# The chunk mask of the attention as a 97th row of queries and keys, in place of a VectorE memset of the scores

## The chip, the cores and the metric

The kernel runs on one core of a Trainium2 chip. The metric is the device time of one execution in microseconds (us), as the median of several runs. TensorE (PE in the profile, PEld for its weight loads), VectorE (DVE), ScalarE (ACT), GpSimd (POOL) and the queue that issues DMAs (SP) run side by side and meet at semaphores.

## The reference, cut to what matters

One layer: RMS norm, a combined projection, three groups of heads side by side (a gated delta rule, a pooling, a softmax attention), an output projection, and a SwiGLU. The change touches only the attention, 4 heads over 1024 tokens with queries and keys of 96 elements:

```python
for qs in range(0, s, Q_BLOCK):                     # Q_BLOCK = 128
    end = qs + Q_BLOCK
    scores = einsum('bqhd,bkhd->bhqk', qf[:, qs:end], kf[:, :end])
    mask = (arange(end) // CHUNK)[None, :] <= ((qs + arange(Q_BLOCK)) // CHUNK)[:, None]    # CHUNK = 64
    p = softmax(where(mask, scores, -inf), axis=-1)
    outs.append(einsum('bhqk,bkhd->bqhd', p, vf[:, :end]))
```

A tile of 128 queries sees all keys up to its own end, except that its first 64 queries must not see its last 64 keys.

## The kernel before, in words

The program is written by hand, engine by engine; what runs beside what is set by the order of the code on each engine and by semaphores. It has four parts: the input projection with its preparations (to about 322 us of the span), four rounds of attention and delta rule (325 to 567 us), the output projection, and the SwiGLU.

A **round** computes one attention head and two chunks of the delta rule. A list `ORDER`, the same for every engine, interleaves the stages of both; the first round is unrolled (`FIRST_ROUND`), rounds 2 to 4 are a loop of each engine (`Fori`). In a round the attention goes through the eight query tiles t = 7 down to 0. A tile's scores have (t + 1) x 128 key columns and lie in two banks of PSUM (4 and 5):

- stage `att_s`: PE multiplies the tile's 96 rows of `qh` by those of `kT` (L2140), in one matmul for up to 512 keys, in two above; every float32 matmul shows as two passes in the trace. VectorE then writes -1e30 into the 64 x 64 corner of the scores (memset, L1756), takes the row maximum (L1758) and negates it (L1760). ScalarE takes the exponential with that bias (L1241, with the row sum).
- stage `att_t`: PE transposes the probabilities by groups of four key tiles (L2156), ScalarE copies them to SBUF (L1247).
- stage `att_pv`: PE multiplies them by V (L2168), VectorE divides by the row sum (L1764, L1767).

The matmuls of L2067 and L2072, and VectorE's L1692 to L1744, are the delta rule's. L2088 opens a chunk of it. `sig` and `gafter` are the signal after an instruction and the wait for a named one: VectorE's maximum waits for the memset's signal (`mask{t}`), since the engine's own writes are to be waited for too.

Ahead of the rounds, POOL sets `n_base` (L948, L949), on which VectorE's small triangular inverses (L1633, L1636) start; these end where the rounds begin for VectorE. Rows 0 to 95 of `kT` are loaded once (`kT_loaded`), those of `qh` once for each head.

Of the kernel before, what the change touches and what calls it, by code (L numbers as in the profile page):

```python
# [30 lines left out]
P = 128  # L31
QK = NOPE + ROPE
# [41 lines left out]
def hybrid_block(nc, e_d, a_d, diag_d, n_d, qkv_d, qk_d, x2_d, hid_d, hs_d, wt_d, x, positions, attn_norm, w_in, conv_w, a_log, dt_bias, gdn_out_norm, pool_w, pool_scale,  # L74
# [206 lines left out]
    with ctx:  # L281
        def sem(name):
            return ctx.enter_context(nc.semaphore(name))
# [71 lines left out]
        qkv_kept = [sem(f"qkv_kept{s}") for s in range(2)]  # L355
        qk_kept = [sem(f"qk_kept{s}") for s in range(2)]
        kT_loaded = sem("kT_loaded")
        pool_moved = sem("pool_moved")
        lat_squared = sem("latents_squared")
        lat_summed = sem("latents_summed")  # L360
# [29 lines left out]
        for t in q_tiles:  # L390
            for g in groups_of[t]:
                head_part.append(("att_t", (t, g), 0))
                if t > 0 and g == groups_of[t][-1]:
# [5 lines left out]
                   ahead=True)  # L399
        td = Steps(sem("att_dve"), [f"{n}{w if st == 'att_s' else w[0]}" for st, w, _ in head_part  # L400
                                    if st == "att_s" or st == "att_pv" and w[1] == groups_of[w[0]][-1]
                                    for n in (("mask", "rowmax", "max") if st == "att_s" else ("rinv", "o"))],
                   ahead=True)


# [18 lines left out]
        def heads_of(m):  # L424
            return m[:, :].unsqueeze(1).broadcast_to([P, 4, P])
# [457 lines left out]
        def _(pool):  # L883
# [52 lines left out]
            for pair in PREP_AT.values():  # L936
                for c in pair:
                    if c >= 2:
                        pool.wait_ge(decay_summed, c - 1)
                    pool.tensor_tensor(gtg[c % 2][:, :, :], heads_of(gt), per_head(g_log[:, c, :]), ALU.mult).then_inc(gtg_ready, 1)  # L940
                for c in pair:
                    pool.wait_ge(key_ss, c + 1)
                    pool.tensor_tensor(k_len[:, c, :], k_ss[c % 2][:, 0, :], half_pos[:, 0:4], ALU.pow).then_inc(key_len, 1)
                for c in pair:
                    pool.wait_ge(decay_exp, c + 1)
                    pool.tensor_tensor(pE[c % 2][:, :, :], pE[c % 2][:, :, :], heads_of(le), ALU.mult).then_inc(decay_masked, 1)
            pool.wait_ge(raw_used, M_GATE + 2)
            link(pool.memset(n_base[:, :, :], 0.0))  # L948
            pool.memset(n_base[:, :, :].rearrange("p i j -> p (i j)")[:, 0:BASE * BASE:BASE + 1], 1.0).then_inc(n_started, 1)  # L949
# [435 lines left out]
        def _(dve):  # L1385
# [43 lines left out]
            def sig(c, ins):  # L1429
                ins.then_inc(c.sem, 1)  # L1430
# [232 lines left out]
            def stages(order, rnd):  # L1663
# [7 lines left out]
                for stage_name, b, back in order:  # L1671
# [30 lines left out]
                    elif stage_name == "yz1":  # L1702
                        gafter(gp[b], "y1")
                        gsig(dve.tensor_tensor(n_[:, 1, :, :], n_[:, 0, :, :], bank_w, ALU.subtract))
                        gafter(gp[b], "z1")
                        gsig(dve.tensor_tensor(m_[:, :, :], m_[:, :, :], bank_u, ALU.subtract))
                    elif stage_name == "yz2":
                        gafter(gp[b], "y2")
                        gsig(dve.tensor_tensor(n_[:, 0, :, :], n_[:, 1, :, :], bank_w, ALU.subtract))
                    elif stage_name == "ks":  # L1710
                        gafter(gp[b], "ks")
                        gsig(dve.tensor_tensor(e[:, :, :], bank_u, per_head(decay(0, b)), ALU.mult))
                        own("r0")
                        gsig(dve.tensor_tensor(e[:, :, :], Vn[b][:, :, :], e[:, :, :], ALU.subtract))
                        gafter(gp[b], "qs")
                        gsig(dve.tensor_tensor(bm[:, :, :], bank_w, per_head(decay(0, b)), ALU.mult))
                    elif stage_name == "tr":
                        gafter(gp[b], "tr")
                        gsig(dve.tensor_tensor(a[:, :, :], bank_u, per_head(
                            k_inv[:, chunk_at, :].rearrange("p a h -> p (a h)")), ALU.mult))  # L1720
                    elif stage_name == "av":
                        gafter(gp[b], "ds")
                        gafter(gg[b], "sd")
                        gsig(dve.tensor_tensor(S_[:, :, :], S_[:, :, :], bank_w, ALU.add))
                        own("o1")
                        gsig(dve.tensor_tensor(m_[:, :, :], bm[:, :, :], bank_u, ALU.add))
                    elif stage_name == "oms":

                        gafter(ga[b], "osq")
                        gsig(dve.tensor_reduce(sc[:, 24:28], Vn[b][:, :, :], axis=AX.X, op=ALU.add))  # L1730
                        own("osum")
                        gsig(dve.scalar_tensor_tensor(sc[:, 28:32], sc[:, 24:28], 1.0 / GDN_DIM, sc[:, 36:40],
                                                      ALU.mult, ALU.mult))
                        own("oms0")
                        gsig(dve.tensor_scalar(sc[:, 28:32], sc[:, 28:32], EPS, None, ALU.add))
                    elif stage_name == "on":
                        gafter(gg[b], "pow")
                        gsig(dve.tensor_tensor(sc[:, 40:44], sc[:, 32:36], sc[:, 12:16], ALU.mult))
                        own("of")
                        gsig(dve.tensor_tensor(n_[:, 1, :, :], m_[:, :, :], per_head(sc[:, 40:44]), ALU.mult))  # L1740
                    elif stage_name == "ot":
                        gafter(gp[b], "ot")
                        tile = ds(i * (2 * P) + b * P, P)
                        gsig(dve.scalar_tensor_tensor(oT[:, ds(i * 2 + b, 1), 0:4, :].rearrange("p t k n -> p (t k) n"),  # L1744
                                                      bank_u, cols[:, C_GDN:C_GDN + 1], sgT[:, :, tile],
                                                      ALU.mult, ALU.mult))
                    elif stage_name == "att_s":
                        t, w = b, (b + 1) * P
                        gafter(tp, f"s{t}")
                        if t < TT - 1:  # L1750
                            gafter(ta, f"e{t + 1}")
                        else:
                            gafter(ta, "e0", i - 1)
                        s2 = ps[:, 4:6, :].rearrange("p a n -> p (a n)")

                        sig(td, dve.memset(s2[0:CHUNK, w - CHUNK:w], BIG_NEG))  # L1756
                        gafter(td, f"mask{t}")
                        sig(td, dve.tensor_reduce(row_stats[t % 2][:, 3:4], s2[:, 0:w], axis=AX.X, op=ALU.max))  # L1758
                        gafter(td, f"rowmax{t}")
                        sig(td, dve.tensor_scalar(row_stats[t % 2][:, 0:1], row_stats[t % 2][:, 3:4], -1.0, None, ALU.mult))  # L1760
                    elif stage_name == "att_pv" and b[1] == groups_of[b[0]][-1]:
                        t = b[0]
                        gafter(ta, f"e{t}")
                        sig(td, dve.reciprocal(row_stats[t % 2][:, 2:3], row_stats[t % 2][:, 1:2]))  # L1764
                        gafter(td, f"rinv{t}")
                        gafter(tp, f"pv{t}.{b[1]}")
                        sig(td, dve.tensor_scalar(V[:, t, ds(i, 1), :].rearrange("p a d -> p (a d)"),  # L1767
                                                  ps[:, 7, 0:V_DIM], row_stats[t % 2][:, 2:3], None, ALU.mult))
                    elif stage_name == "w_low":
                        k, half = ds(i * 2 + b // 2, 1), slice(b % 2 * BANK, (b % 2 + 1) * BANK)  # L1770
                        dve.wait_ge(w_out_high, i * 4 + (b + 1))
                        dve.tensor_tensor(w_out_lo[:, k, half].rearrange("p a n -> p (a n)"),
                                          w_out_sb[:, k, half].rearrange("p a n -> p (a n)"),
                                          w_out_hi[:, k, half].rearrange("p a n -> p (a n)").bitcast(f32),
                                          ALU.subtract).then_inc(w_out_ready, 1)
# [127 lines left out]
        def _(pe):  # L1903
# [153 lines left out]
            for c_ in (gp[0], gp[1], tp):  # L2057
                pe.sem_inc(c_.sem, len(c_.names))
            pe.wait_ge(kT_loaded, 16)
            def stages(order, rnd):  # L2060
                def gafter(c, name, rnd=None):
                    pe.wait_ge(c.sem, c.after(name, i if rnd is None else rnd))
# [12 lines left out]
                for stage_name, b, back in order:  # L2075
# [55 lines left out]
                    elif stage_name == "att_s":  # L2131
# [4 lines left out]
                        else:  # L2136
                            gafter(ta, f"e{t + 1}")
                        for h in range(-(-w // BANK)):
                            n = min(BANK, w - h * BANK)
                            last = pe.matmul(ps[:, 4 + h, 0:n], qh[0:QK, t * P:(t + 1) * P],  # L2140
                                             kT[0:QK, ds(i, 1), h * BANK:h * BANK + n].rearrange("p a n -> p (a n)"),
                                             start=True, stop=True)
                        last.then_inc(tp.sem, 1)
                    elif stage_name == "att_t":
                        t, g = b
# [184 lines left out]
```

## Time and profile before

| | us |
|---|---|
| median of 3 runs | 1325.63 |
| lowest and highest | 1322.32, 1327.6 |
| the profiled execution's own time | 1325.09 |
| its span in the trace | 1322.8 |
| PE busy | 1256.4 (95%) |
| VectorE busy | 834.3 (63%) |
| ScalarE busy | 471.1 (36%) |
| POOL busy | 400.0 (30%) |

The span runs from the first to the last instruction; 2.3 us of the profiled execution's time lie around it. An engine's busy time doesn't say what bounds a stage: that is read from the waits and from the chain of work that ended last, which follows each step back to what released it.

### The profile page before, as it was taken

To read this page: it belongs to the slowest core of one execution; us is meant where nothing else is said; L and a number is where in the kernel's file an instruction comes from. 1 tells how busy PE (TensorE), PEld (TensorE's weight loads), DVE (VectorE), ACT (ScalarE), POOL (GpSimd) and SP (SyncE) were. 2 spreads that over 40 slices of the span, in tenths; PEclk is the share of its full clock that TensorE was granted. 3 is DMA by queue.
4 is the path that set the end of the run, shared out by engine and by line. 5 is a ranking of instruction groups with operands and counts; after the bars stand their busy time and mean duration, and the time that the engine had idled before them with its cause. 6 is when DMAs were issued, how large, how long until landed. Compare 5 with 4: busy or idle time off the path is not lost.

```text
span 1322.8 us, 17456 instructions
## 1 busy us (share of the span) xinstructions
PE 1256.4 (95%) x6156; PEld 1038.5 (79%) x6156; DVE 834.3 (63%) x1324; ACT 471.1 (36%) x776; POOL 400.0 (30%) x367
## 2 busy tenths in 40 slices
PE   6999999998898988899979999999999998999998
PEld 6787777886787776778867888888888886888887
DVE  5446877877365656645385566556655668686776
ACT  5232223342333333324344333333333343344342
POOL 5001111430121112100463655666566445200000
PEclk9998999999798889999989999999999998999999
DMA  7311333537531212004212665565468339575644
GB/s 222 111 49 32 111 97 104 175 121 200 178 85 51 77 50 60 0 9 167 96 54 85 204 199 192 175 222 176 149 215 281 127 97 314 179 234 138 200 118 169
DMA packets 188982, 182.64 MB, mean 138 GB/s; under 512 B 19486, under 2 KB 145772, under 8 KB 188908
## 3 DMA queue, kind: packets, MB, share of 16 engines
q1 hardware_dynamic: 188784, 181.64, 43.6%
q8 instruction: 44, 0.72, 0.2%
q14 instruction: 30, 0.25, 0.1%
q10 hardware_dynamic: 124, 0.04, 0.0%
HBM read 123.97 MB, written 56.62 MB: 137 GB/s over the span
## 4 chain that ended last, share of the span: by engine, by line
PE 69%; DVE 17%; issue 6%; ACT 3%; POOL 2%; DMA 1%; SPq 0%; DVEq 0%; ACTq 0%; POOLq 0%
PE ps L2284 31%; PE ps L2289 14%; PE ps L2067 5%; PE ps L2197 5%; PE ps L1944 4%; PE ps L2140 3%; DVE stage L1545 2%; PE ps L2168 2%; PE ps L1922 2%; DVE w_lo L1426 1%; PE ps L2156 1%; DVE row_stat L1758 1%; DVE wop_lo L1825 1%; DVE stage L1539 1%; POOL mla_sc L931 1%
## 5 line engine op out<-in xcount | busy, mean ns | idle before, releaser
L2284 PE MATMUL ps<-xop,wop_hi 128*128 128x512 f32 x1232 | 381.3, 391 | 6.9 <-issue 4.3
L2284 PEld LDWEIGHTS ps<-xop,wop_hi 128*128 128x128 f32 x1232 | 231.9, 189 | 56.8 <-issue 6.2
L2284 PE MATMUL ps<-xop,wop_lo 128*128 128x512 f32 x616 | 240.4, 390 | 0.0
L2289 PE MATMUL ps<-dop,wop_hi 128*128 128x512 f32 x440 | 137.4, 394 | 6.2 <-DVE x L1897 6.2
L2284 PEld LDWEIGHTS ps<-xop,wop_lo 128*128 128x128 f32 x616 | 116.1, 188 | 24.3
L1825 DVE TENSOR_TENSOR wop_lo<-w_sumS,wop_hi 128x512 fp32r<-128x512 f32 (+1 forms) x104 | 86.6, 835 | 72.4 <-ACT wop_hi L1306 72.4
L1825 DVE TENSOR_TENSOR wop_lo<-w_pair,wop_hi 128x512 fp32r<-128x512 f32 (+1 forms) x78 | 85.2, 1096 | 38.6 <-ACT wop_hi L1306 38.6
L1897 DVE TENSOR_TENSOR x<-x,ps 128x512 f32<-128x512 f32 x112 | 76.6, 684 | 44.3 <-PE ps L2289 44.2
L1944 PE MATMUL ps<-act_hi,w_hi 128*128 128x512 f32 x320 | 104.3, 407 | 0.2 <-DVE stage L1545 0.2
L2289 PEld LDWEIGHTS ps<-dop,wop_hi 128*128 128x128 f32 x440 | 82.9, 190 | 25.7 <-DVE wop_lo L1825 5.8
L1944 PE MATMUL ps<-act_lo,w_hi 128*128 128x512 f32 x320 | 99.5, 392 | 0.0
L1944 PE MATMUL ps<-act_hi,w_lo 128*128 128x512 f32 x320 | 99.5, 392 | 0.0
L2289 PE MATMUL ps<-dop,wop_lo 128*128 128x512 f32 x220 | 86.3, 392 | 0.0
L1306 ACT ACTIVATE wop_hi<-w_sumS 128x512 fp32r<-128x512 f32 (+1 forms) x104 | 63.3, 609 | 63.4 <-PE ps L2284 41.2
L1944 PEld LDWEIGHTS ps<-act_hi,w_hi 128*128 128x128 f32 x320 | 60.3, 191 | 16.2 <-issue 4.7
L1944 PEld LDWEIGHTS ps<-act_lo,w_hi 128*128 128x128 f32 x320 | 60.8, 190 | 13.0
L1944 PEld LDWEIGHTS ps<-act_hi,w_lo 128*128 128x128 f32 x320 | 60.6, 189 | 12.8
L1306 ACT ACTIVATE wop_hi<-w_pair 128x512 fp32r<-128x512 f32 (+1 forms) x78 | 47.4, 612 | 65.0 <-PE ps L2284 53.7
L1426 DVE TENSOR_TENSOR w_lo<-raw,w_hi 128x1024 fp32r<-128x1024 f32 x20 | 27.0, 1350 | 59.4 <-ACT w_hi L1121 59.4
L1025 POOL TENSOR_TENSOR w_sumS<-w_pair 128x512 f32<-128x512 f32 (+1 forms) x26 | 33.6, 1291 | 74.8 <-DVE wop_lo L1825 61.9
L1241 ACT ACTIVATE probs<-ps,row_stat 128x1024 f32<-128x1024 f32 (+7 forms) x32 | 23.7, 741 | 89.9 <-DVE row_stat L1760 89.9
L2168 PEld LDWEIGHTS ps<-V,probsT 128*128 128x128 f32 x288 | 39.8, 206 | 14.4 <-issue 6.8
(308 smaller groups left out, 2340.5 us busy)
## 6 DMA issues: line engine op xcount, KB each, us to landing
w_pair<-in_w_gate_up SPq DMA_DIRECT2D x44, 512.0 KB, 5.3
hidden<-up SPq DMA_DIRECT2D x22, 512.0 KB, 3.0
wd_rows<-in_w_down SPq DMA_DIRECT2D x22, 512.0 KB, 5.4
raw<-in_w_in SPq DMA_DIRECT2D x21, 512.0 KB, 4.4
wd_raw<-down_sums SPq DMA_DIRECT2D x12, 768.0 KB, 8.2
down_sums<-wd_rows SPq DMA_DIRECT2D x33, 256.0 KB, 2.6
wd_raw<-in_w_down SPq DMA_DIRECT2D x9, 768.0 KB, 7.1
qkv_kept<-qkv_st SPq DMA_DIRECT2D x12, 512.0 KB, 5.3
```

The costliest lines, as they stand in the source:

```text
L1025: pool.tensor_tensor(s1, a21, a22, ALU.add).then_inc(sums_ready, 1)
L1306: act.activation(wop_hi[q % RING][:, 0:kh, :], src, ACT.Copy).then_inc(wop_high, 1)
L1426: dve.tensor_tensor(w_lo[slot][:, :, :], raw[rawslot][:, :, :], w_hi[slot][:, :, :].bitcast(f32), ALU.subtract).then_inc(raw_used, 1)
L1825: dve.tensor_tensor(wop_lo[q % RING][:, 0:kh, :], src, wop_hi[q % RING][:, 0:kh, :].bitcast(f32), ALU.subtract).then_inc(wop_ready, 1)
L1897: dve.tensor_tensor(part, part, bank, ALU.add).then_inc(added, 1)
L1944: last = pe.matmul(ps[0:rows, pair + h, :], w[:, k, 0:rows], a[:, k, h * BANK:(h + 1) * BANK], start=(k == 0 and w is whi and a is a_hi), ...
L2067: last = pe.matmul(ps[:, out_bank, h * P:(h + 1) * P], lhs(h), rhs(h), start=True, stop=True)
L2140: last = pe.matmul(ps[:, 4 + h, 0:n], qh[0:QK, t * P:(t + 1) * P], kT[0:QK, ds(i, 1), h * BANK:h * BANK + n].rearrange("p a n -> p (a n)") ...
L2168: last = pe.matmul(ps[:, 7, 0:V_DIM], probsT[0][:, j, :], V[:, kt, ds(i, 1), :].rearrange("p a d -> p (a d)"), start=(kt == 0), stop=(kt = ...
L2197: last = pe.matmul(ps[:, op_pair[t] + h, :], o, w[:, k, h * BANK:(h + 1) * BANK], start=(k == 0 and len(parts) == 2 and w is w_out_hi), st ...
L2284: last = pe.matmul(ps[:, bank, :].rearrange("p (t n) -> p t n", n=P), w[:, k, :], a[:, k, :, :], start=(p in ("P1", "P2", "P7") and k == 0 ...
L2289: last = pe.matmul(ps[:, bank, :], w[:, k, :], a[:, k, :], start=(p in ("P1", "P2", "P7") and k == 0 and w is wop_hi[s] and a is hi), stop ...
```

## The change

The mask becomes part of the product. Row 96 of `kT` is set to 0 for the first 64 and to -1e30 for the last 64 keys of every tile, row 96 of `qh` to 1 for the first 64 and to 0 for the last 64 queries. The product of a query tile with its own key tile (the diagonal block, 128 x 128) then takes 97 rows in place of 96, which adds 1 x -1e30 in just the masked corner. Keys ahead of the diagonal block are still multiplied with 96 rows, so the scores of a tile now come from matmuls over the t x 128 earlier keys and one over the last 128. The memset on VectorE and the wait for it fall away. POOL fills the two rows once, ahead of `n_base`; PE waits for them ahead of the rounds.

```diff
+            k_halves = kT[QK:QK + 1, :, :].rearrange("p h (t c) -> p (h t) c", c=P)
+            q_halves = qh[QK:QK + 1, :].rearrange("p (t c) -> p t c", c=P)
+            pool.wait_ge(mla_turned, TT)
+            pool.wait_ge(decay_masked, TT)
+            link(pool.memset(k_halves[:, :, 0:CHUNK], 0.0))
+            pool.memset(k_halves[:, :, CHUNK:P], BIG_NEG).then_inc(mask_rows, 1)
+            pool.wait_ge(mask_rows, 1)
+            link(pool.memset(q_halves[:, :, 0:CHUNK], 1.0))
+            pool.memset(q_halves[:, :, CHUNK:P], 0.0).then_inc(mask_rows, 1)
+            pool.wait_ge(mask_rows, 2)
             pool.wait_ge(raw_used, M_GATE + 2)
             link(pool.memset(n_base[:, :, :], 0.0))
...
-                        sig(td, dve.memset(s2[0:CHUNK, w - CHUNK:w], BIG_NEG))
-                        gafter(td, f"mask{t}")
                         sig(td, dve.tensor_reduce(row_stats[t % 2][:, 3:4], s2[:, 0:w], axis=AX.X, op=ALU.max))
...
             pe.wait_ge(kT_loaded, 16)
+            pe.wait_ge(mask_rows, 2)
...
                         for h in range(-(-w // BANK)):
-                            n = min(BANK, w - h * BANK)
-                            last = pe.matmul(ps[:, 4 + h, 0:n], qh[0:QK, t * P:(t + 1) * P],
-                                             kT[0:QK, ds(i, 1), h * BANK:h * BANK + n].rearrange("p a n -> p (a n)"),
-                                             start=True, stop=True)
+                            n = min(BANK, t * P - h * BANK)
+                            if n > 0:
+                                pe.matmul(ps[:, 4 + h, 0:n], qh[0:QK, t * P:(t + 1) * P],
+                                          kT[0:QK, ds(i, 1), h * BANK:h * BANK + n].rearrange("p a n -> p (a n)"),
+                                          start=True, stop=True)
+                        at = t * P % BANK
+                        last = pe.matmul(ps[:, 4 + t * P // BANK, at:at + P], qh[0:QK + 1, t * P:(t + 1) * P],
+                                         kT[0:QK + 1, ds(i, 1), t * P:w].rearrange("p a n -> p (a n)"), start=True, stop=True)
                         last.then_inc(tp.sem, 1)
```

On PE, in the loop of rounds 2 to 4, the order of instructions around tile 7 before the change is this. `ISA` and `REGISTER_ALU` are register operations of the engine's sequencer, in brackets stand the semaphores that a row waits for (`att_act` is ScalarE's in the attention):

```order
L2134 ISA
L2062 ISA [waits head_loaded]
L2140 ISA [waits att_act]
L2140 MATMUL ps<-kT_89,qh_290 128x512
L2140 ISA
L2140 MATMUL ps<-kT_89,qh_290 128x512
L2062 REGISTER_ALU
L2062 REGISTER_ALU [waits gdn_dve0]
L2067 MATMUL ps<-S_299,qkvf1_291 128x128 [waits gdn_dve1]
```

And this after it:

```order
L2144 ISA
L2072 ISA [waits head_loaded]
L2151 ISA [waits att_act]
L2151 MATMUL ps<-kT_89,qh_290 128x512
L2151 ISA
L2151 MATMUL ps<-kT_89,qh_290 128x384
L2155 ISA
L2155 MATMUL ps<-kT_89,qh_290 128x128
L2072 REGISTER_ALU
```

The second 512 keys are split into 384 and 128, with a register operation between them. The same split comes in tiles 6, 5, 3, 2 and 1; in tile 4 (512 and 128 keys before too) and in tile 0 the number of matmuls stays.

On VectorE, at the same tile of the loop, before (`row_stat` holds the row statistics, `att_pe` and `att_dve` are PE's and VectorE's own semaphores in the attention):

```order
L1665 ISA [waits att_pe]
L1756 MEMSET ps 64x64 [waits att_act]
L1665 ISA
L1758 TENSOR_REDUCE row_stat1_74<-ps 128x1 [waits att_dve]
L1665 REGISTER_ALU
L1760 TENSOR_SCALAR row_stat1_74<-row_stat1_74 128x1 [waits att_dve]
L1665 ISA
```

And after:

```order
L1676 ISA
L1676 ISA [waits att_pe]
L1767 TENSOR_REDUCE row_stat1_74<-ps 128x1 [waits att_act]
L1769 TENSOR_SCALAR row_stat1_74<-row_stat1_74 128x1 [waits att_dve]
L1676 ISA
```

The memset and its wait are gone, the maximum takes over the waits for PE and ScalarE, and two register operations go with them. The order of all other work on VectorE, and all of it on ScalarE and in the DMA queue, stays.

## Rows read from the trace of the kernel before

**Rows 1.** The page: the span, and each engine's busy time, share and instructions.

```profile
span 1322.8 us, 17456 instructions
PE 1256.4 (95%) x6156; PEld 1038.5 (79%) x6156; DVE 834.3 (63%) x1324; ACT 471.1 (36%) x776; POOL 400.0 (30%) x367
```

**Rows 2.** Windows: busy time and count by engine, granted clock (PEclk), DMA share, GB/s.

```profile
280.00:325.00 45.00, 43.02 (x190) 34.20 (x189) 31.24 (x70) 14.41 (x15) 5.58 (x6) 1.00 0.53 146
325.00:386.00 61.00, 49.00 (x311) 41.63 (x310) 32.55 (x90) 19.87 (x42) 9.89 (x8) 0.83 0.52 160
386.00:447.00 61.00, 54.02 (x363) 46.56 (x363) 35.97 (x89) 20.06 (x42) 11.55 (x10) 0.91 0.21 59
447.00:507.00 60.00, 53.18 (x355) 45.59 (x353) 35.63 (x87) 20.07 (x42) 11.50 (x10) 0.90 0.21 59
507.00:567.00 60.00, 51.21 (x359) 43.69 (x359) 36.97 (x90) 20.64 (x44) 11.54 (x10) 0.94 0.09 26
```

**Rows 3.** Waits, 328 to 567 us: who waited for whom, total, times, longest.

```profile
ACT probs L1241 <- DVE row_stat L1760: 89.9, 32, 6.9
DVE ps L1756 <- PE ps L2140: 55.9, 15, 9.1
PE ps L2156 <- ACT probs L1241: 17.9, 16, 5.0
```

**Rows 4.** The chain of work that ended last, second round: start, us, what.

```profile
386.58 2.24 PE ps L2140 x4
...
389.13 1.24 DVE row_stat L1758
...
391.99 0.65 PE ps L2156 x4
```

**Rows 5.** The same chain: first and last of 23 row maxima on it.

```profile
329.68 1.24 DVE row_stat L1758
...
562.39 0.30 DVE row_stat L1758
```

**Rows 6.** VectorE in order of time, second round, two tiles.

```profile
388.98 0.11 DVE L1756 MEMSET ps<- 64x64 f32 x1 [2.46 <-PE ps L2140]
389.13 1.23 DVE L1758 TENSOR_REDUCE row_stat<-ps 128x1 f32<-128x1024 f32 x1
...
428.33 0.11 DVE L1756 MEMSET ps<- 64x64 f32 x1
428.47 0.69 DVE L1758 TENSOR_REDUCE row_stat<-ps 128x1 f32<-128x512 f32 x1
```

**Rows 7.** The chain, 420 to 450 us: scores of tiles 3, 2, 0, 7.

```profile
426.24 0.86 PE ps L2140 x2
432.82 0.66 PE ps L2140 x2
441.43 0.24 PE ps L2140 x2
446.31 3.62 PE ps L2140 x4
```

**Rows 8.** Weight loads around tile 4 of the first round (512 and 128 keys).

```profile
359.26 0.19 PEld L2140 LDWEIGHTS ps<-kT,qh 96*128 96x128 f32 x1 [0.24 <-issue]
359.69 0.19 PEld L2140 LDWEIGHTS ps<-kT,qh 96*128 96x128 f32 x1 [0.24 <-issue]
359.80 0.53 PEld L2168 LDWEIGHTS ps<-V,probsT 128*128 128x128 f32 x4
```

**Rows 9.** Line L2140 with count: least/median/most ns, first and last start, forms.

```profile
L2140 PEld LDWEIGHTS ps<-kT,qh x96: 188/191/338, 325.0 to 561.7; 96*128 96x128 f32 x96
...
L2140 PEldq FUSED_REGOPS  x6: 51/51/51, 386.2 to 506.9; - x6
```

**Rows 10.** POOL and then VectorE ahead of the rounds, in order of time.

```profile
291.67 0.95 POOL L948 MEMSET n_base<- 128x1024 f32 x1
...
304.42 0.21 DVE L1633 TENSOR_TENSOR solve_tmp<-u_base,n_base 128x31 f32<-128x31 f32 x1 [9.68 <-DMA u_base<-blocks_kept]
```

More of the change, by code:

```diff
@@ L357, in hybrid_block @@
         kT_loaded = sem("kT_loaded")
+        mask_rows = sem("mask_rows")
         pool_moved = sem("pool_moved")
@@ L401, in hybrid_block @@
                                     if st == "att_s" or st == "att_pv" and w[1] == groups_of[w[0]][-1]
-                                    for n in (("mask", "rowmax", "max") if st == "att_s" else ("rinv", "o"))],
+                                    for n in (("rowmax", "max") if st == "att_s" else ("rinv", "o"))],
                    ahead=True)
```

## The prediction

> **What bounds the kernel now.** I read the page first: PE is busy for 95% of the span [rows 1], so time is lost or won only where PE waits or where it gets more work. The change acts in the four rounds, so I read the windows next, cut at the rounds. In the four of them PE is busy for 49.00, 54.02, 53.18 and 51.21 us of 61, 61, 60 and 60, which leaves 34.6 us in which it stands; in the 45 us ahead of them it leaves only 2 us, and VectorE is busy for 33 to 37 us of each round [rows 2]. So neither engine is full in the rounds: the reader is to see a relay, in which one waits for the other in turn.
>
> The waits say at which hand-over. ScalarE's exponential waits for VectorE's negated maximum 32 times, once for each of the 8 tiles of 4 heads, and PE's transpose L2156 waits for the exponential 16 times, 17.9 us in total, which is half of PE's idle time [rows 3]. VectorE in turn waits 15 times for the score product, at the very memset that the change removes [rows 3]. The chain that ended last shows the relay with its parts: score matmuls 386.58 to 388.82, maximum at 389.13 to 390.37 with the memset just ahead of it, then the exponential's start-up, transposes at 391.99 [rows 4]. Over the four rounds the chain goes through a row maximum 23 times out of 32, between the two of [rows 5]. In the other 9 the maximum is ready early enough, and PE works on the delta rule meanwhile.
>
> **The change part by part.**
>
> *The memset goes.* It lasts 0.11 us [rows 6]. What leaves the relay is the distance from its start to the start of the maximum, since the maximum now starts where the memset did, on the same signals of PE and ScalarE: 0.15 us at 389 us and 0.14 at 428 us [rows 6], whether VectorE had stood idle before it or not. I take 0.145. On the 23 places of the chain [rows 5] that is 23 x 0.145 = 3.3 us. Upper end: all 32, 4.6 us. Lower end: only the 16 at which PE's own row shows the wait for the exponential [rows 3], 2.3 us. I take the chain's 3.3, because it also counts the places where the memset delays the delta rule's work that stands behind it on VectorE. The two register operations that go with it lie ahead of and beside the maximum; the distance above is the same with and without an idle spell before it [rows 6], so I give them nothing. At most they would save as much again as one such operation shows on PE, 0.051 us [rows 9], in 24 looped tiles: 1.2 us.
>
> *The last 128 keys get a matmul of their own.* The columns that PE streams stay the same; six tiles in each head have one matmul more, 24 in all, or 48 passes of [rows 9]'s kind. The trace has all the sizes that a split needs: 512 keys in one matmul took 0.86 us, 384 took 0.66, 128 took 0.24 [rows 7]. Cut in two it is 0.66 + 0.24 = 0.90 in place of 0.86, 0.04 us dearer. The weight loads give a lower price: tile 4 has 512 and 128 keys already, and its loads start 0.43 and then 0.11 us apart [rows 8], which is 512 to 128 with nothing added. I take the middle, 0.02 us for a split, 24 x 0.02 = 0.5 us; ends 0 and 1.0. All of it goes to PE, which is on the chain at most of these places, so nothing hides it.
>
> *One row more in the product.* No row of the trace has a 97-row matmul. Nearest is the change from 128 rows (L2088, L2067, L2168) to 96 and back, which happens at every tile; in [rows 8] the load for L2168 follows the last 96-row one after 0.11 us, no more than a pass of 128 columns. I take 0; the other end is the first rival below.
>
> *A register operation between the matmuls, in the loop.* One for each of six tiles in three rounds, 18 times, 0.051 us each [rows 9]: 0.9 us if PE stood still for it. It stands behind a matmul of at least 128 columns, whose two passes take 0.24 us [rows 7], so PE is still streaming while its sequencer does it. I take 0; upper end 0.9.
>
> *POOL fills the two rows.* Four memsets, 2048 and 2048 elements on one partition of `kT`, 512 and 512 of `qh`. The nearest row fills 1024 elements of each partition in 0.95 us [rows 10], so 5120 elements are about 4.8 us. They stand ahead of `n_base` on POOL, whose memset ended at 292.62 (a small one follows); VectorE first uses it at 304.42, when a DMA released it [rows 10]. That leaves up to 11.8 us of cover, which 4.8 don't fill; if POOL took 3.5 us per 1024 elements in place of 0.95 (17.5 us in all), the inverses and with them VectorE's start in the rounds would come 5.7 us late. Nothing else is queued behind them on POOL before the rounds, and PE's new wait for the rows is long over at 325 us. I take 0.
>
> *Sum.* -3.3 + 0.5 = -2.8 us. Against the profiled execution (1325.09, of which 1322.8 span and 2.3 around it) that is 1322.3; against the median of 1325.63, which lies 0.5 above it, **1322.8 us**. With the ends: at most -4.6 - 1.2 = -5.8, at least -2.3 + 1.0 + 0.9 = -0.4.
>
> **The rivals.** No change that can be measured is anything within 0.5%, 6.6 us, of before; the forecast lies inside it.
>
> *Exposed weight loads (slower).* The split works only if the weight load for the 128-column matmul, and the step from 96 to 97 rows, hide behind the matmul before. If each of the 64 passes of a diagonal block had to wait for its weight load of 0.19 us [rows 9] (32 tiles, two passes), it would be +12.2 us, with -3.3 a net +8.9: 1334.5. It counts as slower once a pass pays more than (6.6 + 3.3) / 64 = 0.15 us. Against it: within L2140 a load of 0.19 us starts before the 0.43 us pass ahead of it is done, for the same 96 rows [rows 8]. For it: no row shows 97 rows. 0.07.
> The Trainium skill (TensorE: Matmul & The Clock Gate, Part 3, The mechanism) says that a weight load overlaps running matmuls only when their row groups differ; by that rule 96 and 97 rows share groups, each added load would be paid, and the outcome would be this rival's. The trace does not agree: loads and matmuls of the same 96 rows overlap in it. The same page elsewhere lets loads go ahead into a background buffer, which is what the rows look like.
>
> *The gain is taken up elsewhere.* A tile's exponential comes 0.145 us earlier, but what PE does next waits for another signal that was as late, for instance the delta rule's results from VectorE. Then only the cost of the split is left: 0 to +1.9, about 1326. For it: 23 steps of a chain are shortened by little each, and a chain that is second by less than 0.145 us takes over. Against it: the waits at L2156 last 1.1 us on average (17.9 us in 16 [rows 3]). 0.17.
>
> *The clock.* In the rounds the granted clock is 0.83, 0.91, 0.90 and 0.94 on average, against 1.00 ahead of them [rows 2], a mix of the two levels, 2.4 and 1.2 GHz, and it is lowest in the round in which PE was busy least (49.00 us of 61). Where it is low, work of PE doubles: tile 7's scores took 3.62 us in one round and 2.24 in another [rows 4, 7], 1.4 us apart. A step earlier or later by 0.145 us can put such a stretch beside other work, in either direction. Three stretches' worth less would be -2.8 - 4.2 = -7.0, 1318.6, which counts as faster: 0.08. As much more would be +1.4, 1327.0, still no change: 0.06. For it: the four rounds do the same work and differ in clock by 0.83 to 0.94, and the three runs of before differ by 5.3 us. Against it: nothing in the change pushes it one way.
>
> *It doesn't do what it says.* The memset is gone from VectorE's order for certain; only a POOL fill that runs slower than 2.3 us per 1024 elements, and so past its cover, would undo the gain (5120 elements in 11.8 us). Little chance, 0.01.
>
> **How the numbers follow.** The forecast (-5.8 to -0.4) has 0.61, the taken-up gain 0.17, the clock 0.08 down and 0.06 up, exposed loads 0.07, the late POOL 0.01. Faster by over 0.5% are the clock downward and 0.02 of the forecast's upper end together with a smaller help of the clock: 0.10. Slower is the exposed loads: 0.07. The rest, 0.83, is no change. The range leaves out the exposed loads and half of the clock's tails: from 1318.6 to 1327.2.
>
> **What the changed kernel's profile would show.** VectorE's maximum waits for PE where the memset did, 32 times, with no memset row. The distance from the end of tile 7's last score pass to the maximum's start, 0.31 us before (388.82 to 389.13 [rows 4]), is about 0.17. PE has 48 passes more; on the chain, tile 3's scores take 0.86 to 0.90 us at full clock and tile 0's stay at 0.24. The loads of the 97-row passes start 0.11 us apart, with no gap of 0.19 us on PE ahead of the pass. POOL's four memsets end before 300 us, and VectorE's inverses still start on the DMA. PE's wait at L2156 for the exponential shrinks by some 2 us. The prediction is wrong if the rounds together become shorter by over 6 us without a change in the granted clock, if 97-row passes stand apart from their neighbours, or if the inverses start late.

## The result and the profile after

The changed kernel takes 1313.0 us (median of 6, 1312.68 to 1315.31), the one before 1326.09 (6 runs, 1320.22 to 1329.46). The ratio is 0.9913, 95% interval 0.9891 to 0.9934: faster by 13.1 us, 0.9%. Forecast were 1322.8 us and a range from 1318.6 to 1327.2; the result lies below it.

The page of the changed kernel, to be read against [rows 1]:

```profile
span 1311.2 us, 17485 instructions
PE 1250.3 (95%) x6204; PEld 1039.2 (79%) x6204; DVE 829.6 (63%) x1292; ACT 471.2 (36%) x776; POOL 404.9 (31%) x371
```

TensorE has 48 passes more, VectorE 32 instructions fewer. The four new memsets on POOL took 4.7 us, as estimated, and `n_base` was set long before VectorE's inverses, which a DMA still released. In order of time, POOL and then VectorE, against [rows 10]:

```profile
291.21 1.81 POOL L952 MEMSET kT<- 1x2048 f32 x1
293.08 1.81 POOL L953 MEMSET kT<- 1x2048 f32 x1
294.95 0.52 POOL L955 MEMSET qh<- 1x512 f32 x1
295.53 0.52 POOL L956 MEMSET qh<- 1x512 f32 x1
296.10 0.96 POOL L959 MEMSET n_base<- 128x1024 f32 x1
...
303.85 0.21 DVE L1644 TENSOR_TENSOR solve_tmp<-u_base,n_base 128x31 f32<-128x31 f32 x1 [9.75 <-DMA u_base<-blocks_kept]
```

The chain of the changed kernel at tile 7 of the second round, against [rows 4] (L2151 are the scores of the earlier keys, L2155 of the last 128; L1767 is the maximum, L1769 the negation):

```profile
384.43 1.61 PE ps L2151 x4
386.04 0.24 PE ps L2155 x2
...
386.40 1.24 DVE row_stat L1767
387.64 0.02 issue
387.66 0.17 DVE row_stat L1769
...
389.27 0.65 PE ps L2170 x4
```

The last pass of the scores ends at 386.28 and the maximum starts at 386.40, 0.12 us later; before it was 388.82 to 389.13, 0.31 us. The saving at this tile is 0.19 us, not the 0.145 between the starts of memset and maximum in [rows 6]: the memset also started later behind its release than the maximum does. The signs of the prediction that speak of waits hold too: TensorE's waits at the transposes for the exponential went from 17.9 us ([rows 3]) to 15.2.

The new passes don't stand apart. Weight loads around tile 4 in the second round, against [rows 8]:

```profile
412.90 0.19 PEld L2155 LDWEIGHTS ps<-kT,qh 97*128 97x128 f32 x1 [0.24 <-issue]
413.33 0.19 PEld L2155 LDWEIGHTS ps<-kT,qh 97*128 97x128 f32 x1 [0.24 <-issue]
413.45 0.75 PEld L2182 LDWEIGHTS ps<-V,probsT 128*128 128x128 f32 x4
```

0.43 and then 0.12 us apart, as with 96 rows. The register operations between the matmuls are there, 18 of them:

```profile
L2155 PEldq FUSED_REGOPS  x18: 46/46/46, 384.2 to 546.7; - x18
```

Now the windows, from the first row maximum to the last, first of the kernel before and then of the changed one (columns as in [rows 2]):

```profile
329.68:562.39 232.71, 202.00 (x1352) 174.14 (x1353) 132.95 (x329) 78.26 (x163) 44.48 (x38) 0.90 0.25 73
```

```profile
328.88:552.60 223.72, 194.54 (x1397) 173.56 (x1398) 129.39 (x299) 77.99 (x163) 44.17 (x38) 0.92 0.25 76
```

Of the 11.6 us between the two spans 9.0 lie here, 0.8 ahead and 1.8 behind. The granted clock rose from 0.90 to 0.92. The 0.8 ahead is read from rows shown: 0.57 us because the DMA released VectorE's inverses earlier (303.85 beside 304.42), and some 0.2 is the memset in front of the very first maximum. For the 9.0 in between two things could have happened: shorter waits, or less time at the lower clock. 24 places with 0.19 us (three of four tiles, as the chain's 23 of 32 in [rows 5]) make 4.6 us only.

The runs point to the clock. Over the 30 executions of the kernel before that went with the first experiments, time and mean granted clock go together: 1315.4 and 1315.6 us at 0.982 and 0.981, 1326.6 to 1328.8 at 0.969 or 0.970, which 13 of them had. The changed kernel's six lie at 0.978 to 0.980. So the kernel before could be nearly as fast as the changed one, and mostly wasn't. At the same clock the two differ by less than their medians do: five of the 61 executions of the kernel before that went with the experiments lie at 0.978 to 0.980 like the changed kernel's six, and took 1316.1 to 1321.3 us (median 1319.2) beside 1313.0, so about 6 us remain.

### The profile page after: what moved, and what is told of

Its sections match the earlier page's. It is cut to its first block, busy times and chain, and to the rows that moved or that the text cites. A ratio compares the mean times of both kernels' runs of the same rounds, so it can differ in the third digit from the quotient of the medians.

```text
span 1311.2 us, 17485 instructions
## 1 busy us (share of the span) xinstructions
PE 1250.3 (95%) x6204; PEld 1039.2 (79%) x6204; DVE 829.6 (63%) x1292; ACT 471.2 (36%) x776; POOL 404.9 (31%) x371
## 4 chain that ended last, share of the span: by engine, by line
PE 68%; DVE 17%; issue 6%; ACT 4%; POOL 3%; DMA 1%; SPq 0%; ACTq 0%; DVEq 0%; POOLq 0%
PE ps L2298 29%; PE ps L2303 14%; PE ps L2077 5%; PE ps L2211 5%; PE ps L1953 4%; DVE stage L1556 2%; PE ps L2151 2%; PE ps L2182 2%; PE ps L1931 2%; DVE wop_lo L1834 1%; DVE w_lo L1437 1%; PE ps L2170 1%; DVE stage L1550 1%; POOL mla_sc L932 1%; DVE row_stat L1767 1%
## 5 line engine op out<-in xcount | busy, mean ns | idle before, releaser
L1767 DVE TENSOR_REDUCE row_stat<-ps 128x1 f32<-128x1024 f32 (+7 forms) x32 | 24.2, 757 | 51.9 <-PE ps L2155 51.7
```

## The experiments

Theory **R** (relay): the product, the memset, the maximum, the exponential and the transposes are a relay, on TensorE's path at about 24 of 32 tiles; what leaves it is gained there, and the clock then falls less often. Rivals: **S**, the split matmuls keep TensorE busier and raise the clock; **M**, something of the memset itself; **W**, the waits alone, without the clock. The part of R that speaks of the clock is called **C** where it is tested by itself.

### One part alone, and one part undone

`e1_split`: only the split.

```diff
-                            n = min(BANK, w - h * BANK)
+                            n = min(BANK, t * P - h * BANK)
...
+                        last = pe.matmul(ps[:, 4 + t * P // BANK, at:at + P], qh[0:QK, t * P:(t + 1) * P],
+                                         kT[0:QK, ds(i, 1), t * P:w].rearrange("p a n -> p (a n)"), start=True, stop=True)
```

> The kernel before with one part of the change: the last 128 keys of a tile get a matmul of their own, with 96 rows; memset and mask stay as before. Theory R (relay): the change gains only because the memset leaves VectorE's chain, which is worth about 4 us of pure waiting, and the rest of the 13 us came with fewer stretches at the lower clock. Then this kernel gains nothing: 0 to +1 us over before (1326 to 1327 beside 1326), all waits as before. Theory S (split): the extra matmuls on TensorE are what changed, by keeping it busier, so that the clock falls less. Then this kernel shows a higher granted clock (0.978 or more against 0.973) and at least half of the gain, 1320 or less.

Measured: 1324.88 us beside 1326.36, ratio 0.9989 (0.9964 to 1.0013).

`e2_nomask`: only the memset and its wait gone; the scores stay unmasked, so this kernel leaves a part of the computation out.

```diff
-                        sig(td, dve.memset(s2[0:CHUNK, w - CHUNK:w], BIG_NEG))
-                        gafter(td, f"mask{t}")
```

> The kernel before without the memset and its wait, and nothing in its place: the scores stay unmasked, so this part of the computation is left out. TensorE's matmuls are those of before. Theory R: all of the gain is here, 1312 to 1315 us beside 1326, with the granted clock at about 0.978. Theory S: only the pure waiting, 3 to 4 us, is gained: 1322, clock as before.

Measured: 1313.21 us beside 1326.36, ratio 0.9915 (0.9878 to 0.9953), as the changed kernel.

`e3_twice`: the memset and its wait twice.

```diff
+                        sig(td, dve.memset(s2[0:CHUNK, w - CHUNK:w], BIG_NEG))
+                        gafter(td, f"again{t}")
```

> The kernel before with the memset done twice, each with its own signal and wait, so the relay is longer by another 0.145 us at each of 32 tiles. Theory R: at least +3 us of waiting, and more if the clock falls further: 1329 to 1336 us. If the relay's length is proportional to the time, as a chain without the clock would be, +4 us and a granted clock as before; if the clock does most of it, a step that is not proportional, and a granted clock under 0.973 or unchanged. Theory S: +3 us at most.

Measured: 1331.36 us, ratio 1.0048 (1.003 to 1.0066).

`e4_back`: the changed kernel with the memset put back.

```diff
+                        sig(td, dve.memset(s2[0:CHUNK, w - CHUNK:w], BIG_NEG))
+                        gafter(td, f"mask{t}")
                         sig(td, dve.tensor_reduce(row_stats[t % 2][:, 3:4], s2[:, 0:w], axis=AX.X, op=ALU.max))
```

> The changed kernel (97th row, split matmuls) with the memset and its wait put back in front of the maximum, on scores that are already masked. Theory R: the whole gain is gone, 1326 to 1328 us. Theory S: the gain that the split brought stays, and the memset costs 3 to 5 us: 1316 to 1318.

Measured: 1326.71 us, ratio 1.001 (0.9986 to 1.0034).

S falls: the split alone brings nothing that its interval tells from zero (0.1%, where S asked for 0.5%), and with the memset back the whole gain is gone. The gain is the memset's absence, and the clock goes with it: the median of the granted clock is 0.971 in the kernel before, 0.970 to 0.973 in e1, e3 and e4, and 0.98 in e2. But the gain isn't even: from no memset to one 13 us, from one to two 5. A chain without a second effect would give equal steps. The second step came with hardly any change of the median clock (0.972 beside 0.971); only the better executions are gone, none of the 12 above 0.973 where 8 of 30 were before.

### The clock held up

In the kernel before the clock falls near the opening of a chunk, twice in a round (tiles 4 and 7): TensorE waits and then does four products of one column, eight passes. At tile 4 of the second round the wait is 1.26 us for ScalarE's squares; at tile 7 of the third it is 0.82 us for VectorE's scaling of tile 0 and 0.16 for the squares. Windows of the kernel before around tile 4 and tile 7 of the second and third round (columns as in [rows 2]):

```profile
410.00:414.00 4.00, 2.78 (x23) 2.31 (x21) 1.67 (x4) 2.19 (x5) 0.00 (x0) 1.00 0.02 4
414.00:418.00 4.00, 3.63 (x15) 2.60 (x15) 0.00 (x0) 0.32 (x1) 0.00 (x0) 0.65 0.00 0
418.00:422.00 4.00, 4.00 (x20) 3.97 (x20) 2.86 (x8) 1.57 (x4) 0.70 (x1) 0.50 0.00 0
442.00:446.00 4.00, 3.01 (x26) 2.64 (x24) 3.08 (x9) 1.44 (x5) 0.00 (x0) 0.99 0.32 98
446.00:450.00 4.00, 4.00 (x8) 1.93 (x9) 0.17 (x1) 0.00 (x0) 0.00 (x0) 0.50 0.00 0
```

TensorE is busy for 2.78 and 3.01 of 4 us, and then the clock is at 0.50, its lower level of 1.2 GHz. `e5_before_fill` puts six unused products ahead of the wait for the squares; `e6_after_fill` does it in the changed kernel, `e7_twice_fill` in the one with two memsets. So that it can start, the wait for VectorE (`out`) now stands ahead of the one for ScalarE; both still have to end before the products of one column. This order alone was not run by itself.

```diff
                     if stage_name == "pre":
-                        gafter(ga[b], "sq")
                         gafter(gd[b], "out", i - 1)
+                        for _ in range(6):
+                            pe.matmul(ps[:, U[b], 0:P], ident[:, :], ident[:, :], start=True, stop=True)
+                        gafter(ga[b], "sq")
```

> The kernel before with six 128 x 128 products of the identity with itself put ahead of TensorE's wait for ScalarE's squares at the stage that opens a chunk (L2088, twice a round), into the bank that the stage then overwrites. They add 1.3 us of streaming to a wait of 1.3 us and compute nothing that is used. Theory C (the clock explains what the relay doesn't): TensorE's granted clock falls at these two places of a round, after this patch of little work; filled, it falls there more seldom, the granted clock rises from 0.969 or 0.973 to 0.98 or more, and the time falls to 1313 to 1319 us though the memset is still there. Theory W (waits alone): the time stays at 1326 to 1328, since no wait is shorter, or rises by up to 2 us.

> The changed kernel with the same filling products. Theory C: its clock is high already, so it gains little, 1309 to 1313 us, and the distance to the kernel before with the filling is that of the relay alone, 3 to 5 us. Theory W: the distance to the kernel before with the filling stays at about 13 us.

> The kernel before with the memset done twice and the same filling products. Theory C: the steps from no memset to one and from one to two are equal once the clock is level, each 3 to 5 us, so this run is 3 to 5 us above the one with one memset and the filling. Theory W: as without the filling, 13 us for the first and 5 us for the second.

Measured, beside 1323.98 us of the kernel before: 1317.78 us (ratio 0.9958, 0.9939 to 0.9977), 1312.08 (0.9919, 0.9893 to 0.9945) and 1329.56 (1.0052, 1.0031 to 1.0074). The same windows in `e5_before_fill`, whose rounds lie a few us otherwise, show the higher level of 2.4 GHz throughout:

```profile
410.00:414.00 4.00, 4.00 (x36) 3.89 (x36) 0.64 (x2) 1.59 (x4) 0.00 (x0) 1.00 0.00 0
414.00:418.00 4.00, 3.04 (x21) 2.37 (x21) 1.95 (x6) 0.89 (x2) 0.00 (x0) 1.00 0.00 0
418.00:422.00 4.00, 4.00 (x36) 3.94 (x37) 2.05 (x5) 1.11 (x2) 1.01 (x1) 1.00 0.02 4
442.00:446.00 4.00, 4.00 (x24) 3.10 (x25) 0.57 (x4) 0.00 (x0) 0.00 (x0) 1.00 0.00 0
446.00:450.00 4.00, 2.58 (x22) 2.35 (x21) 3.40 (x6) 1.21 (x2) 1.04 (x1) 1.00 0.12 31
```

What the filling does is seen at tile 7 of the third round, on the chain. The kernel before (products of one column, then the scores, the last row of [rows 7]):

```profile
445.13 1.18 PE ps L2088 x8
```

and `e5_before_fill` (filling, products of one column, scores):

```profile
442.00 1.60 PE ps L2087 x12
443.60 0.79 PE ps L2090 x8
444.39 1.84 PE ps L2142 x4
```

The scores take 1.84 us in place of 3.62, at a granted clock of 1.00 in place of 0.50; filling, products and scores together take 4.23 us, beside 4.80 for products and scores before. But the filling stands on the chain here, with its whole 1.60 us: no wait hides it. So it has a price. It shows in the changed kernel with and without the filling, where both have a clock of 1.00: from the last row maximum of the third round to the first of the fourth it takes 6.27 us without the filling and 7.40 with it. The runs show it too: `e5_before_fill` took 1317.2 us and more at a clock of 0.986 to 0.988, while the kernel before took 1315.4 to 1317.0 in its four executions at 0.981 and 0.982.

W falls: work that nobody uses made the kernel before faster by 6.2 us, and this is what the clock gives less what the filling costs. The changed kernel, which had less to regain, gained nothing that the intervals tell (ratio 0.9919 with the filling, 0.9913 without). With the filling the two stand 5.7 us apart. From first to last row maximum, `e5_before_fill` and then `e6_after_fill`:

```profile
329.01:555.80 226.79, 195.34 (x1436) 171.30 (x1437) 133.00 (x329) 78.18 (x163) 44.43 (x38) 0.98 0.25 75
```

```profile
327.85:549.90 222.05, 194.59 (x1481) 174.93 (x1482) 129.40 (x299) 78.10 (x163) 44.23 (x38) 0.98 0.26 77
```

At the same clock, 0.98, and with the same filling, the rounds are 4.7 us apart: that is the relay. One place of it, where VectorE hadn't waited, tile 3 of the second round in `e5_before_fill` (VectorE in order of time):

```profile
425.07 0.16 DVE L1701 TENSOR_TENSOR tok_sc<-tok_sc 128x4 f32<-128x4 f32 x1
425.30 0.11 DVE L1756 MEMSET ps<- 64x64 f32 x1
425.45 0.69 DVE L1758 TENSOR_REDUCE row_stat<-ps 128x1 f32<-128x512 f32 x1
```

and in `e6_after_fill`:

```profile
421.90 0.16 DVE L1712 TENSOR_TENSOR tok_sc<-tok_sc 128x4 f32<-128x4 f32 x1
422.08 0.69 DVE L1767 TENSOR_REDUCE row_stat<-ps 128x1 f32<-128x512 f32 x1
```

0.38 us from the instruction before to the maximum, against 0.18: here the memset costs 0.20 us, 0.15 behind its start and 0.05 ahead of it.

The third run is where theory C, as it was put, missed: the step from one memset to two should have been 3 to 5 us with the filling and was 11.8. Its trace shows that the relay's own step is even. In the third round, where all three filled kernels have a granted clock of 1.00, the starts of the successive row maxima of `e7_twice_fill` lie 9.89, 8.47, 9.92, 9.74, 6.11, 3.97, 3.81 and 7.78 us apart, 59.69 in all, against 58.43 in `e5_before_fill` and 57.34 in `e6_after_fill`: 1.26 us for the second memset and 1.09 for the first, so 5.0 and 4.4 for four rounds. The chain of the kernel with two memsets goes through all 32 row maxima, that of the other two through 27 and 23. What is more than that goes with the clock: the filling lifted it, but not to the same level. The median run of `e7_twice_fill` has a granted clock of 0.982 where `e5_before_fill` has 0.988, and its run at 0.986 took 1324.8 us, 5 to 6 above the three of `e5_before_fill` at 0.986 (1318.9 to 1320.1). What makes the clock fall more often there was not looked for.

### Another step out of the same relay

`e8_flip_before` keeps the memset and takes the negation out: the scores get the opposite sign, so the row minimum is the bias itself. `e9_flip` does it to the changed kernel, `e10_flip_fill` adds the filling.

```diff
-BIG_NEG = -1.0e30
+BIG_NEG = 1.0e30
...
-                dve.tensor_scalar(sc[:, 32:36], sc[:, 24:28], lat_rstd[:, 2 * t:2 * t + 1], float(QK) ** -0.5,
+                dve.tensor_scalar(sc[:, 32:36], sc[:, 24:28], lat_rstd[:, 2 * t:2 * t + 1], -float(QK) ** -0.5,
...
-                        sig(td, dve.tensor_reduce(row_stats[t % 2][:, 3:4], s2[:, 0:w], axis=AX.X, op=ALU.max))
-                        gafter(td, f"rowmax{t}")
-                        sig(td, dve.tensor_scalar(row_stats[t % 2][:, 0:1], row_stats[t % 2][:, 3:4], -1.0, None, ALU.mult))
+                        sig(td, dve.tensor_reduce(row_stats[t % 2][:, 3:4], s2[:, 0:w], axis=AX.X, op=ALU.min))
...
-                                       bias=row_stats[t % 2][:, 0:1], accum_out=row_stats[t % 2][:, 1:2]).then_inc(ta.sem, 1)
+                                       bias=row_stats[t % 2][:, 3:4], scale=-1.0, accum_out=row_stats[t % 2][:, 1:2]).then_inc(ta.sem, 1)
```

> The kernel before, memset kept, but with another step taken out of the same relay: the queries are scaled by -1 where they are scaled anyway, so the scores have the opposite sign, VectorE takes the row minimum and ScalarE uses it as its bias with a scale of -1; the negation L1760 (0.15 us, some 0.2 with its hand-over) falls away. Theory R (length of the relay counts, whichever step leaves it, by 0.19 us at 24 of 32 tiles, and the clock follows): as good as the changed kernel, 1311 to 1316 us, granted clock about 0.979. Theory M (something of the memset itself: its write into the scores' banks, its two waits): less than half of the gain, 1320 or more.

> The changed kernel with the negation gone too, in the same way (the mask row is +1e30 then). Theory R: the relay is shorter by another 0.2 us at 24 tiles, 4.5 to 5 us: 1306 to 1309 us, if the clock stays at 0.979. Theory M: the negation is hidden, 1312 to 1313.

> The same with the six filling products at the opening of a chunk. Theory R: the filled series is even: one memset 1317.8, none 1312.1, so this one 1306 to 1308. If it is no faster than the one without filling, the clock has nothing left to give in the rounds at this relay length.

Measured, beside 1325.0 us of the kernel before: 1311.21 us (ratio 0.99, 0.9878 to 0.9922), 1307.85 (0.9876, 0.9855 to 0.9897) and 1305.5 (0.9859, 0.9835 to 0.9882). M falls: with the memset still there, a step of the same size elsewhere in the relay brings as much as the change, with a clock of 0.979 to 0.982. The next step brings some 5 us more (1313.0 to 1307.85, ratios 0.9913 and 0.9876) at a clock of 0.980 (median), as the changed kernel had. The filling adds 2.4, a little more than was expected (1305.5 beside 1306 to 1308); since it has a price of its own, this doesn't say how much the clock has left to give. `e9_flip` beats both kernels by taking work away, `e10_flip_fill` is the fastest version run. The page of `e10_flip_fill`:

```profile
span 1303.7 us, 17652 instructions
PE 1247.1 (96%) x6300; PEld 1039.9 (80%) x6300; DVE 823.7 (63%) x1260; ACT 470.3 (36%) x776; POOL 405.5 (31%) x371
```

## Why the prediction was wrong

**What bounds the rounds: right.** The relay is the path at three tiles of four. The runs e2, e3, e4 and e8 show that its length counts. The filled pair shows where: in the second round the starts of successive row maxima lie 9.70, 8.38, 9.72, 9.56, 5.91, 3.97, 3.62 and 7.60 us apart in `e5_before_fill` and 9.51, 8.40, 9.54, 9.36, 5.68, 4.03, 3.43 and 7.41 in `e6_after_fill`, so six of the eight steps are shorter, by about 0.2 us each.

**The memset goes: the right mechanism, mis-sized.** The term was 23 x 0.145 = 3.3 us. The count holds as a size: six steps of eight are 24 in four rounds, though the chains that the traces show go through 18 maxima in the changed kernel, 27 and 23 in the filled pair. A place is worth 0.19 to 0.20, since the distance from the memset's start to the maximum's left out that the memset starts 0.05 us later behind its release than the maximum. The prediction gave the two register operations nothing; on the chain one of 0.05 us more stands ahead of tile 7's memset in the looped rounds than ahead of the maximum. But at tile 7 of the unrolled first round, where the chain shows no register operation, the gain is as large (from the end of the instruction before to the maximum 0.27 us, then 0.04), so whose the 0.05 is stays open. Measured at the same clock and with the same filling: 4.7 us in the rounds, 5.7 between the medians.

**The last 128 keys, 0.5 us: small, as forecast.** e1 and e4 can't tell it from zero, so they don't confirm the 0.5 either. The 97th row costs nothing that shows, the register operations neither, and the loads overlap, so the slower rival was wrong. The rule of the Trainium skill (TensorE: Matmul & The Clock Gate, Part 3, The mechanism) that was cited beside it, read alone, doesn't hold in these runs: the first 97-row load runs under a pass of 96 rows, and behind the second the next load starts 0.12 us later, less than the 0.19 us that a load takes and as far apart as the passes of 128 columns.

**POOL: right**, 4.7 us under 11.8 of cover.

**The clock: the step that failed.** The rival "the clock" said that "nothing in the change pushes it one way", priced three stretches and gave them 0.08; in the sum the clock stood at nothing. The clock did follow the change: with the relay shorter, the changed kernel's six runs lay at 0.978 to 0.980, where before 13 of 30 runs lay at 0.970 or below. Of the 13.1 us, 5.7 are the relay by the filled pair; the other 7.4 are the clock's by difference. Two numbers from elsewhere agree: the two kernels are about 6 us apart at equal clock, and the filling gave 6.2 us to the kernel before with the memset in place, its own cost already taken off. The spread of the runs before, 1322.3 to 1327.6, and the round clocks of 0.83 to 0.94 stood in the prediction; they were taken as noise of both signs. Its price for a stretch was low too: the 2.24 us that it set beside 3.62 was itself a mix (clock 0.79), and at the higher level these scores take 1.84. What the runs put in its place: out of the kernel before, less idle time of TensorE in the rounds, by either way (a shorter relay or the filling), raised the median clock, from 0.971 to 0.973 to about 0.98 without the memset or the negation, and to 0.988 with the filling. It isn't a rule for every step: with both gone the median was 0.980, no higher than with one of them gone (0.979 to 0.982), and the second memset without the filling left the median at 0.972.

**Taken up elsewhere: this rival was wrong**, by the same six steps of eight.

**What stays open.** Why in the kernel before so many runs share one low clock, what exactly decides between a run at 0.982 and one at 0.969, and why the filling held the clock less well with two memsets. 1.8 us of the difference between the two profiled spans lie behind the last row maximum, where the two programs are the same; no run was made for them, nor for the DMA that came 0.57 us earlier.

## What to carry to other kernels

Where TensorE works in short bursts between waits, as in these rounds, an instruction on another engine can cost more than its length: its hand-over at each place of the chain, and the lower clock that the added idle time may bring. Read the granted clock of each run before the change; if the runs spread with it, give a forecast of the clock the sign of the change in idle time, and a chance to match. Then try what costs nothing: a sign or a scale moved into work that is done anyway. Unused products in a wait after which TensorE's clock falls can pay as well, but look on the chain whether the wait hides them.

## What was not expected of the hardware

- Executions of one and the same program differed by 13 us (1315.4 to 1328.8), in step with a mean granted clock of 0.982 to 0.969, and 13 of 30 sat at the low end.
- 48 products that nobody uses (6 at 8 places of the rounds) made the kernel 6.2 us faster, though they stood on the chain of work themselves (1.60 us at tile 7 of the third round).
- A 64 x 64 memset of 0.11 us cost 0.19 to 0.20 us at a place of the chain.
- POOL filled one partition at the pace of 128: 1.81 us for 2048 elements on one, 0.96 for 1024 on each of 128.
